# RWKV-7 low-rank products moved to two row halves of TensorE and two PSUM banks

## The chip, the cores and the metric

The kernel runs on one core of a Trainium2 chip. The metric is device microseconds of one execution. The engines are named as the profile names them: PE is TensorE, PEld its weight loads, ACT is ScalarE, DVE is VectorE, POOL is GpSimd and SP is SyncE, which issues most transfers. PSUM has eight banks of 512 fp32 columns; the code calls them bank 0 to bank 7.

## The reference, cut to what matters

The reference is one inference step of a two-layer decoder. Each layer projects its input once, runs three head groups on parts of the result (RG-LRU, RWKV-7 time mixing, latent attention), gates them, and projects back. The change touches only how RWKV-7 gets its decay and its gate `a`:

```python
w_log = -softplus(-(rk_w0 + tanh(xw @ rk_w1) @ rk_w2)) - 0.5
decay = exp(-exp(w_log))
a = sigmoid(rk_a0 + (xa @ rk_a1) @ rk_a2)
# per token t, with k, v, r, kk of the same token
s = s * decay + (s @ -kk) (kk * a)^T + v k^T
o = s @ r
```

Both are low-rank: 256 inputs go to 32 and from 32 to 256. There are 1104 tokens (1040 of one prompt with its meta tokens, 64 of eight samples), width 256, four heads of 64. All arithmetic is fp32.

## The kernel before, in words

Each layer is five blocks one after the other: `project_block`, `rwkv_block`, `prompt_block`, `sample_block`, `output_block`. Within a block each engine has its own instruction list, and the lists meet only in semaphores.

`project_block` computes the input projection (L406), tile of columns by tile of columns, in the order of the list `Z_JOBS`. ACT empties every tile from PSUM. Jobs named "front" are woven in, and they do the first steps of the first RWKV tile: "front" 0 has the first low-rank product (L468) and the key and receptance projections (L479), "front" 1 has the value projection (L479, into `aux[0]`, which is bank 6) and then the second low-rank products of decay and gate (L484, both into `aux[1]`, which is bank 7). ACT copies v out (L555) and takes one tanh over 512 columns (L557).

`rwkv_block` works on nine tiles of 128 tokens. A tile needs a chain of small products (the solve: `prod`, `n2`, `z1`, `z2`, `z3`, `mid`, `zf`, `wu`, `wt`), and a loop over four chunks of 32 tokens through the state: `read` k, an addition on DVE, `write` k, an update of the state on DVE (L1535), `read` k + 1. All engines walk through one order written by hand, `RWKV_ORDER`: behind each solve stage of tile t stand steps of neighbouring tiles, listed in `BESIDE`. Behind `prod` of tile t are the first low-rank product and the first projection of tile t + 1; behind `n2` are

```python
"n2": [("proj", 1, 1), ("lora", 1, 0), ("write", -1, 0)],
```

that is, the second projection of tile t + 1 (`proj`, L1020), the low-rank products of decay and gate of tile t + 1 (`lora`, L1026), and the first state write of tile t - 1 (`write`, L1207 and L1209, into columns 0 to 127 of bank 4). The tiles that `lora` handles here are 1 to 8; tile 0 comes from `project_block`.

`lora` takes from `low` two blocks of 32 rows, `tw[0:32, 0]` (tanh, for decay) and `tw[0:32, 1]` (a copy, for the gate), with a row of ones under each that adds the bias (`LORA + 1` = 33 rows). It multiplies them by `w2` and puts decay into columns 0 to 255 and gate into columns 256 to 511 of bank 7. ACT (L1269) turns the whole bank into `wa` with one tanh. DVE (`decay`, L1402 and L1403) makes `logd` and the gate of it, and `sums` multiplies `logd` by masks on PE.

The weights `w2` come in two loads of SyncE in `project_block` (L364, L365), counted by `m.s_ld` against `N_LD`.

Of the kernel before, what the change touches and what calls it, by code (L numbers as in the profile page):

```python
# [266 lines left out]
def project_block(nc, m):  # L267
# [39 lines left out]
    sq = {"ckv": mixed[:, 4:6, :], "cq": mixed[:, 2:4, :]}  # L307
    one = const[:, C_ONE * P:(C_ONE + 1) * P]
    N_PAR = 16 * 6
    N_LD = 16 * 6  # L310
    rw = rwkv_weights(m)

    def span(g):
# [6 lines left out]
    with nc.Block() as block:  # L320
        @block.sync
        def _(sp):
            def weights(i):
                if i >= 2:

                    sp.wait_ge(s_z, Z_LOADS[i - 1])
                w = z_weights(m, i)
                a = Z_AT[Z_LOADS[i]]
                sp.dma_start(w, m.w_z[layer, :, :, a:a + w.shape[2]]).then_inc(s_w[i], 16)

            if layer == 0:
                w0, n0 = z_weights(m, 0), Z_AT[2]
                for c in range(4):
                    k = slice(2 * c, 2 * c + 2)
                    sp.dma_start(xT[:, k, :], m.xT[:, k, :]).then_inc(m.s_x0[c], 16)
                    sp.dma_start(w0[:, k, 0:n0], m.w_z[0, :, k, 0:n0]).then_inc(m.s_x0[c], 16)
                sp.dma_start(w0[:, :, n0:], m.w_z[0, :, :, n0:Z_AT[Z_LOADS[1]]]).then_inc(m.s_const, 16)
            sp.dma_start(m.pfs[:, :], m.pf[layer]).then_inc(s_par, 16)
            sp.dma_start(lru_w, m.lru_w[layer]).then_inc(s_par, 16)
            sp.dma_start(slru, m.slru[layer]).then_inc(s_par, 16)  # L340
            sp.dma_start(shift, m.sshift[layer]).then_inc(s_par, 16)
            for b2 in range(2):
                sp.dma_start(ua_s[b2][:, :, 0:CX], m.sconv[layer, :, b2]).then_inc(s_par, 16)
            if layer == 0:
                sp.dma_start(const[:, :], m.consts[:, 0:C_N]).then_inc(m.s_const, 16)
                sp.dma_start(m.pages_in[:, :], m.pages_at).then_inc(m.s_const, 16)
            weights(1)
            weights(2)

            sp.wait_ge(s_ze, Z_TILES.index("ub1") + 1)  # L350
            n = 0
            for b2 in range(2):
                sp.dma_start(m.o_conv[layer, :, b2, 0:1, :], ua[:, b2, TP:TP + CX]
                             .rearrange("p (o t) -> p o t", o=1)).then_inc(s_out, 16)
                sp.dma_start(m.o_conv[layer, :, b2, 1:1 + NB, :], ua_s[b2][:, :, TS:TS + CX]).then_inc(s_out, 16)
                n += 2
            weights(3)
            sp.dma_start(rw.prow, m.prow[layer]).then_inc(m.s_ld, 16)
            sp.dma_start(rw.s_in, m.swkv[layer]).then_inc(m.s_ld, 16)
            sp.wait_ge(s_out, 16 * n)  # L360
            sp.wait_ge(s_xc, 2)
            sp.dma_start(rw.w1, m.rk_w1[layer]).then_inc(m.s_ld, 16)
            sp.dma_start(rw.rkw, m.rk_w[layer]).then_inc(m.s_ld, 16)
            sp.dma_start(rw.w2[0:LORA], m.rk_w2[layer]).then_inc(m.s_ld, 16)  # L364
            sp.dma_start(rw.w2[LORA:LORA + 1], m.prow[layer, LORA:LORA + 1, 0:2, :]).then_inc(m.s_ld, 16)  # L365
            sp.wait_ge(s_shift, 2)
            sp.dma_start(m.o_shift[layer], shend).then_inc(s_out, 16)
            sp.wait_ge(s_root, NG)
            sp.dma_start(m.o_ckv[layer], ckv[:, :, :]).then_inc(s_out, 16)
            sp.wait_ge(s_kr, 1)  # L370
            sp.dma_start(m.o_kr[layer], kr[64:64 + ROPE, :]).then_inc(s_out, 16)

            sp.wait_ge(s_h, 2)
            sp.dma_start(m.o_lru[layer], hend).then_inc(s_out, 16)

            sp.wait_ge(s_out, 16 * (n + 4))
# [25 lines left out]
        def _(pe):  # L402
# [19 lines left out]
            for job, i in Z_JOBS:  # L422
# [50 lines left out]
                if job == "front" and i < 2:  # L473
                    for n in ((0, 1), (2,))[i]:
# [5 lines left out]
                                                    rw.rkw[:, k, (1, 0, 2)[n], :], start=k == 0, stop=k == 1)  # L480
                        last.then_inc(s_rkv, 1)
                if job == "front" and i == 1:
                    for j in range(2):
                        last = nc.tensor.matmul(aux[1][:, j * WA:(j + 1) * WA], fw.tw[0:LORA + 1, j, :],  # L484
                                                rw.w2[0:LORA + 1, j, :], start=True, stop=True)
                    last.then_inc(s_lo2, 1)
                if job == "front" and i == 2:
                    pe.wait_ge(s_sg, 1)
# [11 lines left out]
        def _(act):  # L500
# [7 lines left out]
            for job, i in Z_JOBS:  # L508
# [35 lines left out]
                if job == "front" and i == 0:  # L544
                    act.wait_ge(s_lo1, 1)
                    nc.scalar.activation(fw.tw[0:LORA, 0, :], aux[1][0:LORA, 0:P], ACT.Tanh)
                    nc.scalar.copy(fw.tw[0:LORA, 1, :], aux[1][LORA:2 * LORA, 0:P]).then_inc(s_lo1e, 1)
                    act.wait_ge(s_rkv, 1)
                    nc.scalar.activation(fw.k_sb, aux[0][:, 0:WA], ACT.Copy,
                                         scale=const[:, C_ROW:C_ROW + 1]).then_inc(s_rkve, 1)  # L550
                    act.wait_ge(s_rkv, 2)
                    nc.scalar.copy(fw.r_sb, aux[1][:, 0:WA]).then_inc(s_rkve, 1)
                if job == "front" and i == 1:
                    act.wait_ge(s_rkv, 3)
                    nc.scalar.copy(fw.v_sb[:, 0], aux[0][:, 0:WA]).then_inc(s_rkve, 1)  # L555
                    act.wait_ge(s_lo2, 1)
                    nc.scalar.activation(fw.wa, aux[1], ACT.Tanh, scale=0.5).then_inc(s_lo2e, 1)  # L557
                if job == "front" and i == 2:
                    act.wait_ge(s_kk, 1)
                    for h in range(H_B):  # L560
# [34 lines left out]
        def _(dve):  # L595
# [110 lines left out]
            def both(x):  # L706
                return x.rearrange("p (o n) -> p o n", o=1).to_broadcast([P, 2, WA])

            nc.vector.memset(fw.tw[LORA:LORA + 1, :, :], 1.0)
            a = PF["mix"][0]  # L710
            link(nc.vector.tensor_scalar(fw.rest, m.pfs[:, a:a + 10], -1.0, 1.0, ALU.mult, ALU.add))
            dve.wait_ge(m.s_ld, N_LD)
# [36 lines left out]
SOLVE = ["prod", "n2", "z1", "z2", "z3", "mid", "zf", "wu", "wt"]  # L749
BESIDE = {  # L750
    "prod": [("low", 1, 0), ("read", -1, 0), ("proj", 1, 0), ("norm", -2, 0)],
    "n2": [("proj", 1, 1), ("lora", 1, 0), ("write", -1, 0)],
    "z1": [("read", -1, 1), ("proj", 1, 2), ("decay", 1, 0), ("centre", -2, 0)],
    "z2": [("write", -1, 1), ("sums", 1, 0), ("finish", -2, 0)],
    "z3": [("read", -1, 2), ("keys_norm", 1, 0)],
# [37 lines left out]
def rwkv_block(nc, m):  # L793
# [156 lines left out]
            if stage in stages:  # L950
                stages[stage](t, k)

    N_LD = 16 * 6
    with nc.Block() as block:
        @block.sync
        def _(sp):
# [40 lines left out]
        def _(pe):  # L997
# [25 lines left out]
            def lora(t, _):  # L1023
                pe.wait_ge(s_lo1e, t + 1)
                for i in range(2):
                    last = nc.tensor.matmul(bank[7][:, i * WA:(i + 1) * WA], tw[0:LORA + 1, i, :], w2[0:LORA + 1, i, :],  # L1026
                                            start=True, stop=True)
                last.then_inc(s_lo2, 1)

# [151 lines left out]
            def write(t, k):  # L1181
                if k >= len(steps(t)):
                    return
                n = steps_to(t) + k
                pe.wait_ge(s_u, n + 1)
                pe.wait_ge(s_hat, t + 1)
                if n >= 1:
                    pe.wait_ge(s_state, n + 1)
                if of_samples(t, k):
                    pe.wait_ge(s_pl, 2)  # L1190
                    pe.wait_ge(s_um, 1)
                    pe.wait_ge(s_wu, RT)
                    for hf in range(2):
                        for i, x in enumerate((um, vm)):
                            for c in range(2):
                                for p in range(2):
                                    last = nc.tensor.matmul(
                                        bank[4 + c][64 * p:64 * p + 64, hf * 2 * P:(hf + 1) * 2 * P],
                                        bk[rows(2 + c), t % 3, i, head(hf, p)], x[rows(2 + c), :, head(hf, p)],
                                        start=i == 0, stop=i == 1)  # L1200
                    last.then_inc(s_wr, 1)
                    return
                for i, c in enumerate(steps(t)[k]):
                    for hf in range(2):
                        for p in range(2):
                            out = bank[4][64 * p:64 * p + 64, i * P + hf * HD:i * P + (hf + 1) * HD]
                            nc.tensor.matmul(out, bk[rows(c), t % 3, 0, head(hf, p)],  # L1207
                                             u[rows(c), hf, p * HD:(p + 1) * HD], start=True, stop=False)
                            last = nc.tensor.matmul(out, bk[rows(c), t % 3, 1, head(hf, p)],  # L1209
                                                    v_sb[rows(c), t % 3, head(hf, p)], start=False, stop=True)  # L1210
                    last.then_inc(s_wr, 1)
# [31 lines left out]
        def _(act):  # L1243
            bank = m.bank

            def low(t, _):
                act.wait_ge(s_lo1, t + 1)
                nc.scalar.activation(tw[0:LORA, 0, :], bank[7][0:LORA, 0:P], ACT.Tanh)
                nc.scalar.copy(tw[0:LORA, 1, :], bank[7][LORA:2 * LORA, 0:P]).then_inc(s_lo1e, 1)

            def proj(t, n):
                act.wait_ge(s_rkv, 3 * t + n + 1)
# [12 lines left out]
            def lora(t, _):  # L1265
                act.wait_ge(s_lo2, t + 1)
                if t >= 1:
                    act.wait_ge(s_sg, t)
                nc.scalar.activation(wa, bank[7], ACT.Tanh, scale=0.5).then_inc(s_lo2e, 1)  # L1269

            def sums(t, _):
                act.wait_ge(s_kk, t + 1)
# [1359 lines left out]
```

## Time and profile before

| | |
|---|---|
| median of three runs | 2076.92 us (2073.3 to 2080.65) |
| the profiled execution | 2072.72 us, span 2070.9 us |
| PE / PEld busy over the span | 93% / 60% |
| DVE / ACT / POOL busy | 50% / 31% / 11% |
| projection block, layers 0 and 1 | about 0 to 282 and 1040 to 1320 us |
| RWKV block, layers 0 and 1 | about 282 to 470 and 1320 to 1510 us |
| mean granted PE clock | 0.975 of full speed |

The span runs from the first to the last instruction. A fp32 matmul of the program shows as two MATMUL rows (and two LDWEIGHTS rows) in the trace, so a count of 4 at L1026 is one pair of products. The duration of a MATMUL row includes the time for which it flows through the array and overlaps with the next row, so the time that a group takes from PE is read from its start to the start of the next group. Tiles of the program that live in the one large buffer all appear as `work`, and so groups are told apart by their lines.

### The profile page before, as it was taken

The numbers are of one execution on the slowest core, as the hardware profiler recorded it, in microseconds if no ns is written. First come the engines' busy times: TensorE is split into PE (matmuls) and PEld (weight loads), VectorE is DVE, ScalarE is ACT, GpSimd is POOL, SyncE is SP. The second block draws the span as 40 slices with busy tenths as digits, with TensorE's granted clock in tenths as the row PEclk, the third lists the DMA queues.
The fourth block names the chain that finished last, engine by engine and source line by source line (L and its number), as shares of the span: only waits on it lengthen the run. The fifth ranks groups of instructions, "written<-read, shape, count | busy, mean of one in ns | idle before, by whom it ended". The sixth has DMA issues, their size and how long they took to land. (4 is left out here: it accounts for less than half of the span.)

```text
span 2070.9 us, 50992 instructions
## 1 busy us (share of the span) xinstructions
PE 1934.8 (93%) x22434; PEld 1248.1 (60%) x22434; DVE 1031.0 (50%) x2399; ACT 643.5 (31%) x1711; POOL 223.2 (11%) x223
## 2 busy tenths in 40 slices
PE   8999989988999999999989999899889999999997
PEld 5665667775566567754446656677755665677443
DVE  2017127775566468833330071277755664688333
ACT  1222234442455432310012222344424554322000
POOL 0000001010000034202100000001100000442022
PEclk9999999997999989999999999999979999999999
DMA  6102010000000367731121020100000002677121
GB/s 213 51 1 91 1 48 4 4 4 23 1 1 10 83 232 270 260 129 61 67 64 51 1 92 0 48 4 4 4 23 1 1 14 79 244 272 266 62 81 53
DMA packets 50112, 151.13 MB, mean 73 GB/s; under 512 B 15138, under 2 KB 19490, under 8 KB 40420
## 3 DMA queue, kind: packets, MB, share of 16 engines
q1 hardware_dynamic: 37604, 72.36, 10.5%
q0 software_dynamic: 12288, 75.51, 9.8%
q8 instruction: 178, 2.92, 0.6%
q14 instruction: 42, 0.34, 0.1%
HBM read 130.27 MB, written 12.86 MB: 69 GB/s over the span
## 5 line engine op out<-in xcount | busy, mean ns | idle before, releaser
L406 PE MATMUL psum<-work 128*128 128x368 f32 x1536 | 484.6, 476 | 8.9 <-DMA work<-w_z 6.6
L406 PEld LDWEIGHTS psum<-work 128*128 128x128 f32 x1536 | 293.6, 192 | 193.7 <-issue 8.2
L2465 PE MATMUL psum<-work,mixed 128*128 128x512 f32 (+1 forms) x576 | 248.8, 592 | 1.6 <-PEq L2137 1.6
L2465 PEld LDWEIGHTS psum<-work,mixed 128*128 128x128 f32 (+1 forms) x576 | 106.2, 186 | 137.7 <-issue 137.7
L2333 DVE STREAM_TRANSPOSE work<-work 128x1024 f32<-128x1024 f32 x128 | 150.5, 1214 | 0.3 <-issue 0.2
L1906 ACT ACTIVATE work<-psum,work 128x128 f32<-128x128 f32 (+8 forms) x130 | 98.0, 754 | 160.6 <-DVE work L2015 160.4
L1786 PE MATMUL psum<-work 96*128 96x512 f32 (+3 forms) x384 | 139.1, 495 | 2.3 <-ACT work L1906 2.1
L2077 POOL DMA_INDIRECT work<-cache_ckv,pages x64 | 60.7, 948 | 606.9 <-PE psum L1740 377.7
L2237 PE MATMUL psum<-work,ckv 128*64 128x256 f32 x1024 | 117.6, 382 | 0.7 <-ACT ckv L2292 0.7
L2513 DVE SCALAR_TENSOR_TENSOR work<-work,psum 128x512 f32<-128x512 f32 (+1 forms) x36 | 23.1, 683 | 162.1 <-PE psum L2465 162.1
L1786 PEld LDWEIGHTS psum<-work 96*128 96x128 f32 x384 | 67.4, 189 | 60.0 <-issue 43.5
L2014 DVE TENSOR_REDUCE work<-psum 128x1 f32<-128x128 f32 (+8 forms) x130 | 99.5, 765 | 4.5
L651 DVE TENSOR_TENSOR mixed<-work 128x1104 f32<-128x1104 f32 x4 | 5.2, 1307 | 193.6 <-ACT work L579 193.5
L1797 PE MATMUL psum<-const_sb,work 128*128 128x128 f32 x594 | 84.9, 276 | 13.7 <-ACT work L1915 13.1
L2237 PEld LDWEIGHTS psum<-work,ckv 128*64 128x64 f32 x1024 | 71.6, 137 | 42.8 <-issue 11.3
L1915 ACT COPY work<-psum 128x512 f32<-128x512 f32 (+1 forms) x166 | 84.2, 546 | 23.3 <-PE psum L1797 22.5
L1797 PEld LDWEIGHTS psum<-const_sb,work 128*128 128x128 f32 x594 | 67.0, 141 | 38.9 <-issue 18.2
L1733 PE MATMUL psum<-cq,work 128*128 128x368 f32 x192 | 72.6, 510 | 11.1 <-DVE work L1965 7.6
L1815 PE MATMUL psum<-work 128*64 128x128 f32 x1152 | 81.9, 280 | 0.0
L2013 DVE TENSOR_TENSOR psum<-psum,const_sb 128x128 f32<-128x128 f32 (+1 forms) x130 | 38.2, 294 | 87.3 <-PE psum L1786 72.7
L523 ACT ACTIVATE mixed<-psum 128x368 f32<-128x368 f32 x48 | 19.4, 477 | 183.3 <-PE psum L406 183.3
L2282 ACT ACTIVATE work<-psum,work 128x1024 f32<-128x1024 f32 x32 | 35.7, 1115 | 130.5 <-DVE work L2344 130.5
(311 smaller groups left out, 2953.0 us busy)
## 6 DMA issues: line engine op xcount, KB each, us to landing
work<-w_z SPq DMA_DIRECT2D x4, 2560.0 KB, 11.0
work<-w_out SPq DMA_DIRECT2D x4, 2048.0 KB, 8.8
xres<-work SPq DMA_DIRECT2D x16, 512.0 KB, 2.9
work<-xT SPq DMA_DIRECT2D x4, 1104.0 KB, 8.8
work<-x_tok SPq DMA_DIRECT2D x8, 512.0 KB, 4.0
work<-xres SPq DMA_DIRECT2D x8, 512.0 KB, 4.3
work<-w_z SPq DMA_DIRECT2D x1, 2304.0 KB, 13.9
o_ckv<-ckv SPq DMA_DIRECT2D x2, 1104.0 KB, 4.3
```

The source lines that it names most:

```text
L406: return nc.tensor.matmul(zb[i % 2][n][:, 0:G], z_weights(m, g)[:, k, lo:lo + Z_W[i]], xT[:, k, span(n)], start=k == 0, stop=k == DK - 1)
L1733: last = nc.tensor.matmul(bank_of(j)[:, 0:G], wuq[:, k, h, :], cq[:, k, span(g)], start=k == 0, stop=k == 1)
L1786: last = nc.tensor.matmul(m.bank[2 * u + b][:, 0:w], qt[0:96, p % 2, u, t * P:(t + 1) * P], kt[0:96, p % 2, u, a:a + w], start=True, stop= ...
L1797: last = nc.tensor.transpose(m.bank[4 + at % 2][0:w, n * P:(n + 1) * P], pr[:, i % 2, u * N_FULL * P + c * P:u * N_FULL * P + c * P + w], ...
L1815: last = nc.tensor.matmul(m.bank[6][u * VD:(u + 1) * VD, 0:P], val[:, c, (2 * p + u) * VD:(2 * p + u + 1) * VD], pT[:, i % 2, n * P:(n + 1 ...
L1906: nc.scalar.activation(pr[:, i % 2, u * N_FULL * P:u * N_FULL * P + keys(i)], scores_of(i, u), ACT.Exp, bias=mx[:, 2 * (i % 2) + u:2 * (i ...
L1915: nc.scalar.copy(pT[0:w, i % 2, 4 * g * P:(4 * g + len(c)) * P], m.bank[4 + at % 2][0:w, 0:len(c) * P]).then_inc(s_pte, 1)
L2014: link(nc.vector.tensor_reduce(sm, scores_of(i, u), AX, ALU.max))
L2077: pool.indirect_dma_start(rows[n % RING][:, s, :], None, m.cache_ckv, row).then_inc(m.s_pg[n % RING], 16)
L2237: last = nc.tensor.matmul(m.bank[6 + n % 2][64 * s:64 * s + 64, 0:R], pT[:, n % 2, j, 64 * s:64 * s + 64], pgc[n % RING][:, s, j * R:(j + ...
L2333: last = nc.vector.transpose(kt[:, half, s], pgc[n % RING][:, s, :].rearrange("p (j k n) -> p j k n", j=KEYS, k=2) [:, :, half, :])
L2465: last = nc.tensor.matmul(yb[t % 2][half][0:n, :], m.mixed[:, k, lo:lo + n], wo[half][:, k, :], start=k == 0, stop=k == DK - 1)
```

## The change

The two low-rank products get different rows of the array and different banks. The gate's operands (`tw[..., 1, :]` and `w2[..., 1, :]`, with the row of ones and the bias row) move from partitions 0 to 32 to partitions 64 to 96. Decay's product stays in bank 7, columns 0 to 255; the gate's goes to columns 256 to 511 of another bank: bank 4 in `rwkv_block`, `aux[0]` (bank 6) in `project_block`. From this follow:

- Tanh is taken in two passes of 256 columns instead of one of 512.
- `w2` and its bias row arrive in four loads instead of two, and the memset of ones is two.
- In `project_block`, PE waits before the pair until ACT has copied k, r and v out (`s_rkve` 3), since v is read from the bank that the gate's product writes.
- In `rwkv_block`, the first state write of a tile (k = 0, bank 4) waits until the tanh of the low-rank products issued before it is done (`s_lo2e`), and `lora` now stands before the second projection in the order.

```diff
-    N_LD = 16 * 6
+    N_LD = 16 * 8
...
-            sp.dma_start(rw.w2[0:LORA], m.rk_w2[layer]).then_inc(m.s_ld, 16)
-            sp.dma_start(rw.w2[LORA:LORA + 1], m.prow[layer, LORA:LORA + 1, 0:2, :]).then_inc(m.s_ld, 16)
+            for j in range(2):
+                r = 2 * LORA * j
+                sp.dma_start(rw.w2[r:r + LORA, j], m.rk_w2[layer, :, j]).then_inc(m.s_ld, 16)
+                sp.dma_start(rw.w2[r + LORA:r + LORA + 1, j], m.prow[layer, LORA:LORA + 1, j, :]).then_inc(m.s_ld, 16)
...
                 if job == "front" and i == 1:
+                    pe.wait_ge(s_rkve, 3)
                     for j in range(2):
-                        last = nc.tensor.matmul(aux[1][:, j * WA:(j + 1) * WA], fw.tw[0:LORA + 1, j, :],
-                                                rw.w2[0:LORA + 1, j, :], start=True, stop=True)
+                        r = slice(2 * LORA * j, 2 * LORA * j + LORA + 1)
+                        last = nc.tensor.matmul(aux[1 - j][:, j * WA:(j + 1) * WA], fw.tw[r, j, :],
+                                                rw.w2[r, j, :], start=True, stop=True)
...
-                    nc.scalar.activation(fw.wa, aux[1], ACT.Tanh, scale=0.5).then_inc(s_lo2e, 1)
+                    for j in range(2):
+                        w = slice(j * WA, (j + 1) * WA)
+                        last = nc.scalar.activation(fw.wa[:, w], aux[1 - j][:, w], ACT.Tanh, scale=0.5)
+                    last.then_inc(s_lo2e, 1)
...
-            nc.vector.memset(fw.tw[LORA:LORA + 1, :, :], 1.0)
+            for j in range(2):
+                nc.vector.memset(fw.tw[2 * LORA * j + LORA:2 * LORA * j + LORA + 1, j, :], 1.0)
...
-    "n2": [("proj", 1, 1), ("lora", 1, 0), ("write", -1, 0)],
+    "n2": [("lora", 1, 0), ("proj", 1, 1), ("write", -1, 0)],
...
             def lora(t, _):
                 pe.wait_ge(s_lo1e, t + 1)
                 for i in range(2):
-                    last = nc.tensor.matmul(bank[7][:, i * WA:(i + 1) * WA], tw[0:LORA + 1, i, :], w2[0:LORA + 1, i, :],
+                    r = slice(2 * LORA * i, 2 * LORA * i + LORA + 1)
+                    last = nc.tensor.matmul(bank[(7, 4)[i]][:, i * WA:(i + 1) * WA], tw[r, i, :], w2[r, i, :],
                                             start=True, stop=True)
...
+                if k == 0:
+                    pe.wait_ge(s_lo2e, min(t + 3, RT))
...
-                nc.scalar.copy(tw[0:LORA, 1, :], bank[7][LORA:2 * LORA, 0:P]).then_inc(s_lo1e, 1)
+                nc.scalar.copy(tw[2 * LORA:3 * LORA, 1, :], bank[7][LORA:2 * LORA, 0:P]).then_inc(s_lo1e, 1)
...
-                nc.scalar.activation(wa, bank[7], ACT.Tanh, scale=0.5).then_inc(s_lo2e, 1)
+                for i in range(2):
+                    w = slice(i * WA, (i + 1) * WA)
+                    last = nc.scalar.activation(wa[:, w], bank[(7, 4)[i]][:, w], ACT.Tanh, scale=0.5)
+                last.then_inc(s_lo2e, 1)
```

## Rows read from the trace of the kernel before

**Rows 1.** Busy time of each engine in the RWKV block, layer 0; granted clock

```profile
core 0: us, PE busy (x) PEld busy (x) DVE busy (x) ACT busy (x) POOL busy (x), PEclk, DMA share, GB/s
...
282.00:470.00 188.00, 169.54 (x5250) 136.78 (x5240) 131.56 (x460) 86.97 (x301) 17.42 (x16) 0.97 0.04 14
```

**Rows 2.** Timeline of one RWKV tile, layer 0: start, us, engine, line

```profile
306.07 1.13 PE L1020 MATMUL psum<-work 128*128 128x256 f32 x4
306.18 0.37 ACT L1315 COPY work<-psum 128x256 f32<-128x256 f32 x1 [0.18 <-PE psum L1089]
...
307.13 1.13 PE L1026 MATMUL psum<-work 33*128 33x256 f32 x4
...
308.19 0.34 PE L1207 MATMUL psum<-work 32*64 32x64 f32 x4
308.29 0.60 ACT L1269 ACTIVATE work<-psum 128x512 f32<-128x512 f32 x1 [0.68 <-PE psum L1026]
```

**Rows 3.** PE by line and shape: count, busy us, mean ns

```profile
L2465 PE MATMUL psum<-work,mixed 128*128 128x512 f32 x512 | 221.2, 592 | 1.6 <-PEq L2137 1.6
L2237 PE MATMUL psum<-work,ckv 128*64 128x256 f32 x1024 | 117.6, 382 | 0.7 <-ACT ckv L2292 0.7
...
L2206 PE MATMUL psum<-work,ub 32*64 32x256 f32 x2048 | 66.6, 396 | 0.0
...
L1026 PE MATMUL psum<-work 33*128 33x256 f32 x64 | 18.0, 402 | 0.0
```

**Rows 4.** Timeline of the same tile: state reads whose halves differ in rows

```profile
303.54 0.31 PE L1171 MATMUL psum<-work 64*32 64x64 f32 x4
...
303.68 0.28 PE L1174 MATMUL psum<-work 64*32 64x64 f32 x4
...
303.79 0.30 PE L1171 MATMUL psum<-work 64*32 64x64 f32 x4
```

**Rows 5.** Timeline: narrow products in two row halves; ScalarE copies before them

```profile
321.62 1.07 ACT L1292 COPY work<-psum 128x512 f32<-128x512 f32 x2 [0.30 <-PE psum L1053]
...
322.75 0.86 PE L1065 MATMUL psum<-work 64*32 64x64 f32 x64 [0.51 <-ACT work L1292]
...
323.54 1.09 PE L1006 MATMUL psum<-ub,work 128*64 128x128 f32 x8
```

**Rows 6.** Timeline: four ScalarE passes over 256 columns of PSUM

```profile
314.46 1.21 ACT L1282 ACTIVATE work<-psum 128x256 f32<-128x256 f32 x4 [1.52 <-PE psum L1043]
```

**Rows 7.** What PE waits for, layer 0 from 288 to 456 us

```profile
PE psum L1020 <- DVE work L1460: 5.9, 6, 1.0
```

**Rows 8.** Projection block, layer 0, around its low-rank products: timeline

```profile
202.86 0.27 DVE L709 MEMSET work<- 1x256 f32 x1
...
204.98 1.67 DVE L702 SCALAR_TENSOR_TENSOR work<-work,pfs,ub 128x128 f32<-128x128 f32 x6
...
211.07 1.09 PE L468 MATMUL psum<-ub,work 128*64 128x128 f32 x8
...
229.66 1.03 PE L479 MATMUL psum<-work 128*128 128x256 f32 x4
229.86 1.22 ACT L523 ACTIVATE mixed<-psum 128x368 f32<-128x368 f32 x3 [14.47 <-PE psum L406]
...
230.61 1.13 PE L484 MATMUL psum<-work 33*128 33x256 f32 x4
230.95 0.39 ACT L555 COPY work<-psum 128x256 f32<-128x256 f32 x1
...
231.67 4.60 PE L406 MATMUL psum<-work 128*128 128x368 f32 x14
```

**Rows 9.** SyncE: issue of a small load; a wait behind it

```profile
L364 SPq DMA_DIRECT2D work<-rk_w x2: 429/444/460, 161.5 to 1200.0; - x2
...
SPq L369 <- DVE ckv L663: 9.6, 1, 9.6
```

**Rows 10.** Projection block, ScalarE loading a function table

```profile
248.99 1.28 ACT L567 ACT_TABLE_LOAD   x1
```

More of the change, by code:

```diff
@@ L546, in _ @@
                     nc.scalar.activation(fw.tw[0:LORA, 0, :], aux[1][0:LORA, 0:P], ACT.Tanh)
-                    nc.scalar.copy(fw.tw[0:LORA, 1, :], aux[1][LORA:2 * LORA, 0:P]).then_inc(s_lo1e, 1)
+                    nc.scalar.copy(fw.tw[2 * LORA:3 * LORA, 1, :], aux[1][LORA:2 * LORA, 0:P]).then_inc(s_lo1e, 1)
                     act.wait_ge(s_rkv, 1)
@@ L951, in run @@
                 stages[stage](t, k)
-    N_LD = 16 * 6
+    N_LD = 16 * 8
     with nc.Block() as block:
```

## Prediction

> **What bounds the kernel now.** I read the page first, then the busy time by stretch, then the waits of the stretch that the change touches, then the timeline of one tile in it, and last the timeline of the projection block, where the same pair of products stands once per layer. The reader is to see four things.
>
> In the RWKV block TensorE (PE) is busy for 169.5 of 188 us, and no other engine for more than 131.6 [rows 1]. PE runs one hand-written order, so whatever shortens that order shortens the block, unless a wait further on belongs to another engine's own chain. The decay's and gate's products (L1026) take a PE slot of 308.19 - 307.13 = 1.06 us and nothing else runs in it [rows 2]. A trace row is half of an fp32 product: four rows for two products. Per row, 512 columns take 221.2 / 512 = 0.432 us, so 256 columns take 0.216 [rows 3]. Four of these are 0.864; the other 0.19 us of the slot is the first weight load and the array running empty at its end, and the projection slot beside it (306.07 to 307.13) has the same 1.06 [rows 2]. There are 64 rows of L1026, so 16 pairs in the kernel, eight per layer [rows 3].
>
> **Saved: do the two products overlap?** Before, both use array rows 0 to 32 and write bank 7. Afterwards they stand in rows 0 to 32 and 64 to 96 and write banks 7 and 4. No row of this trace shows two row halves with 128 output columns each, so the gain is bounded from nearby rows. For it: L2206 (32 rows, 64 columns out, 256 in; 2048 rows of that form) takes 66.6 / 2048 = 0.033 us per row against 0.216 alone, 6.6 times less. Column halves alone, as in L2237, give 117.6 / 1024 = 0.115, under 2 times less. So the four row quarters of L2206 do overlap, writing four banks [rows 3]. Row halves in particular: the state reads L1171 and L1174 alternate in the code between the halves and write two banks; the 8 rows from 303.54 to 303.79 take 0.25 us, 0.031 each, where 64 columns alone cost 0.432 / 8 = 0.054 [rows 4]. That is four steps of 0.0625 instead of 0.054, 0.009 lost per step. I take full overlap with that loss: two steps of 0.216 in place of four, 0.432 - 0.02 = **0.41 us saved per pair**, a slot of 0.65. Upper end: no loss, 0.43. Lower end: L1065 is also in row halves, and its 64 rows start over 323.54 - 322.75 = 0.79 us, 0.0123 each, far above 0.054 / 8. Something per row, taken here as the weight load of 64 x 32, is paid one after another there [rows 5]. Four times the columns is 0.05; two of those before the second product starts are 0.10, which leaves 0.33 saved.
>
> A rule is to be weighed here. The rows above show four rows of L1171 (both halves) ahead of four rows of L1174, though the code issues L1171 and L1174 of one half before those of the other; the two halves are interleaved [rows 4]. The Trainium skill ("TensorE: Matmul & The Clock Gate", Part 3, what overlaps and what doesn't) says that matmuls are a strict queue in start and end, without reordering. Read for an fp32 product of two passes, it would let only the first product's second pass run beside the second's first. By the row, two steps are saved; by the rule, one, which is the second rival below.
>
> **Does the saving reach the end?** After the pair come the projection (now behind it), the first state write, z1, the state read and so on. From 306.07 on, PE has no gap until after L1207 [rows 2]. The PE waits further on are short and come from DVE or ACT work which itself follows PE work behind this slot: the largest, L1020 on DVE L1460, is 5.9 us in 6 tiles [rows 7]. DVE's queue up to L1460 goes back through the state updates and reads to the first state write, so the chain and the wait move earlier together. I take all of it: 16 x 0.41 = 6.6 us.
>
> **The new wait of the first state write.** It must wait until both tanh passes are done, because the second product now lies in bank 4 beside the write. Swapping the order puts the projection's 1.06 us between. In tile time: the pair starts at 306.07 and the projection at 306.07 + 0.65 = 306.72. ACT took up the old tanh at 308.29, 0.10 after PE's next slot began, so the new one at 306.82; ACT is free from 306.18 + 0.37 = 306.55 [rows 2]. Two passes over 256 columns: four take 1.21 us [rows 6] and one about 0.37 (the copy of rows 2), so each further one 0.28; two take 0.65, against 0.60 for the one of 512 columns. They end at 307.47, and PE learns it 0.06 later: L1292 ends at 321.62 + 1.07 = 322.69 and L1065 starts at 322.75 [rows 5]. That is 307.53. PE reaches the write at 306.72 + 1.06 = 307.78. Cost 0 with 0.25 us of cover. Were the cover gone, each us of lateness would cost one per tile, since the write, z1 and every read behind it stand in PE's queue, and DVE's state update waits for the write. The projection's copy on ACT follows tanh and its product ends later anyway: 0. Before and after, the stretch has three changes of product shape, and the 0.19 us around a slot was the same for the projection and the pair: 0.
>
> **The projection block.** There the new wait is not covered. PE finishes the value projection (L479) and went on to the pair at 230.61. Now it waits for ACT's copy of v (L555), since the second product goes to the bank which that copy reads. The copy stands behind three gate passes (229.86 + 1.22) and ends at 230.95 + 0.39 = 231.34, plus 0.06 = 231.40: **0.79 us of wait** [rows 8]. The pair then saves 0.41. PE is dense on both sides (L406 follows at 231.67), so net +0.38 per layer, **+0.76** in all. If the pair saves 0.33 to 0.43 it is +0.92 to +0.72.
>
> **Loads and small edits, at nothing.** The low-rank weights arrive in four loads instead of two, so two more issues of 0.43 us on SyncE, and the wait behind them there (output of ckv) lasts 9.6 us anyway [rows 9]. They are issued near 162 us and DVE first uses the weights after 202.86. One memset of 0.27 us becomes two, 0.27 more at most; DVE's preparation ends at 204.98 + 1.67 = 206.65 and PE's first product of it starts at 211.07 [rows 8]. The gate's copy to other partitions keeps its shape.
>
> **Sum.** -6.6 + 0.76 = -5.8 us. With the bounds of the pair: -16 x 0.33 + 0.92 = -4.4 to -16 x 0.43 + 0.72 = -6.2. The profiled execution took 2072.72 us (span 2070.9), so it would take 2066.9. The median of the runs shown, 2076.92, is 4.2 above it, and the same step gives **2071.1** (-0.28%), own range 2070.7 to 2072.5 before scatter; the three runs of before lie up to 3.7 us from their median.
>
> **Rivals.**
> A, the forecast: both steps overlap and all reaches the end. 0.72.
> B, one step only, by program order: 0.22 saved per pair, 16 x 0.22 = 3.5, less 2 x (0.79 - 0.22) = 1.1: -2.4, 2074.5. For it, that no row has 128 columns out in halves; against it, the interleaving [rows 4]. 0.10. (It is also what the page's rule above would give.)
> C, overlap, but the gain is taken back by a wait on DVE: L1020's wait of 1.0 us per tile [rows 7] would grow by 0.41. It would if DVE's chain crossed this slot without touching PE; DVE waits for the first state write, so I see no such chain. 16 x 0.41 gone, +0.76 stays: 2077.7. 0.08.
> D, no overlap at all, as if 128-column products took the whole array: nothing saved, 2 x 0.79 = +1.6: 2078.5. The L2206 row speaks against it [rows 3]. 0.04.
> E, the other side: the state write waits because tanh comes late. It needs ACT to be over 0.25 us later than worked out; the gain is gone at 0.25 + 5.8 / 16 = 0.61 late. Price by a row: a function table load of 1.28 us before tanh [rows 10], 1.03 of stall per tile, 16 x 1.03 - 5.8 = +10.7: 2087.6. Against it: ACT does tanh and copies back to back in this block without such a load [rows 2]. 0.06, half of it for a smaller lateness which only eats the gain.
>
> **How the numbers follow.** About 0.3% (6.2 us) is what a measurement of this kernel can tell from no change. A lies just inside it, so with a scatter of one or two us it falls outside some 45 times in 100: 0.72 x 0.45 = 0.32, and 0.01 from B. Slower by over 0.3%: half of E, 0.03, and 0.02 for scatter on C and D. The rest, 0.62, is within. The range takes A with the runs' scatter below, 2066.5, and reaches over B, C and D above, 2078.5.
>
> **What would show it.** In the profile after: rows of L1026's successor in pairs that start together, its slot at about 0.65 and the tile period shorter by 0.41; the first state write with no idle time ahead of it that ACT releases; in the projection block PE idle about 0.8 us ahead of the pair, released by ACT's copy of v. Wrong would be: a slot of 0.84 (B) or 1.06 (D); PE idle ahead of the write (E); a larger wait on DVE L1460's counterpart with the same period (C).

## The result, and the profile after

| | before | after |
|---|---|---|
| median, first 20 runs each | 2078.82 us | 2072.01 us (2064.13 to 2081.76) |
| ratio after / before, with 95% interval | | 0.9963 (0.9952 to 0.9975) |
| the same kernel again, 12 runs beside 20 of before | 2078.18 us | 2076.18 us, ratio 0.9986 (0.9972 to 1.0000) |
| the profiled execution | 2072.72 us | 2076.18 us, span 2074.4 us |

The change makes the kernel slightly faster. The forecast was -5.8 us, 0.9972. The first comparison says 0.37% less and the second 0.14%; the forecast lies between them, inside the first interval and at the edge of the second. A step of a quarter of a per cent is about as large as the difference between two such series, so its size is read from the traces, piece by piece.

The profiled execution itself is of no use as a total: it is 3.5 us longer than the one of before, the third slowest of its kernel's twenty. Up to the last pair of low-rank products it is ahead (1470.2 against 1476.6 us). Its excess lies in the last 600 us, where almost nothing was changed: from that pair to the end it takes 2074.4 - 1470.2 = 604.2 us, and before it was 594.3. The mean granted clock of this stretch is 0.95 of full speed against 0.97, and 0.02 of 600 us is 12 us (an estimate from two rounded clocks), which is as much as the excess. One such place is near 1932 us, where PE ran at the lower of its two clocks (0.51, against 1.00 at the same place before). Busy time by stretch, after (the number before the last two is the granted clock):

```profile
1470.20:2074.40 604.20, 559.27 (x5961) 345.61 (x5955) 334.10 (x696) 181.42 (x462) 94.60 (x89) 0.95 0.27 94
...
1932.00:1942.00 10.00, 9.13 (x32) 4.89 (x33) 1.56 (x8) 0.00 (x0) 0.00 (x0) 0.51 0.51 197
```

and before:

```profile
1476.64:2070.90 594.26, 550.69 (x5952) 339.52 (x5951) 333.83 (x695) 181.17 (x460) 93.80 (x88) 0.97 0.27 96
...
1938.00:1948.00 10.00, 10.00 (x24) 4.40 (x24) 0.00 (x0) 0.00 (x0) 0.00 (x0) 1.00 0.37 151
```

**One tile of the RWKV block**, timeline of PE after (L1028 is the projection that was L1020, L1035 the pair that was L1026, L1218 the first state write that was L1207):

```profile
306.09 0.67 PE L1098 MATMUL psum<-work 32*32 32x64 f32 x32
306.69 0.70 PE L1035 MATMUL psum<-work 33*128 33x256 f32 x4
307.32 1.13 PE L1028 MATMUL psum<-work 128*128 128x256 f32 x4
308.38 0.34 PE L1218 MATMUL psum<-work 32*64 32x64 f32 x4
...
328.31 0.49 PE L1035 MATMUL psum<-work 33*128 33x256 f32 x2
```

The reader is to see the pair's slot, 307.32 - 306.69 = 0.63 us where it was 1.06 [rows 2], and no idle time in front of the write at 308.38. The tile takes 328.31 - 306.69 = 21.62 us. Before, from 307.13 [rows 2] to the same place of the next tile (timeline of PE before):

```profile
329.17 1.13 PE L1026 MATMUL psum<-work 33*128 33x256 f32 x4
```

22.04 us. So 0.42 us per tile arrives whole at the next tile. Both are the shortest steps of their traces, and several tiles are up to 0.7 us longer in either kernel. Over the six steps of each layer from the second pair to the eighth, the mean falls from 22.16 to 21.76 us, by 0.40. ACT in the same tile, after: copy of the solve's second product, the two tanh passes, copy of the projection.

```profile
306.80 0.37 ACT L1329 COPY work<-psum 128x256 f32<-128x256 f32 x1 [0.19 <-PE psum L1098]
307.44 0.66 ACT L1282 ACTIVATE work<-psum 128x256 f32<-128x256 f32 x2 [0.27 <-PE psum L1035]
308.49 0.37 ACT L1270 COPY work<-psum 128x256 f32<-128x256 f32 x1 [0.39 <-PE psum L1028]
```

Tanh ends at 308.10 and the write may start 0.06 later; PE gets there at 308.38, with 0.22 to spare. What PE waits for, after, layer 0 from 288 to 456 us:

```profile
PE psum L1028 <- DVE work L1474: 5.9, 6, 1.0
PE psum L1074 <- ACT work L1306: 3.8, 8, 0.5
```

The wait for DVE is as long as in [rows 7]: it has moved with the tile and has not grown.

**The projection block**, timeline of PE and of ACT's copy of v after:

```profile
214.30 1.10 PE L481 MATMUL psum<-work 128*128 128x256 f32 x4 [0.66 <-ACT work L553]
...
230.08 1.03 PE L481 MATMUL psum<-work 128*128 128x256 f32 x4
231.81 0.70 PE L488 MATMUL psum<-work 33*128 33x256 f32 x4 [0.71 <-ACT work L559]
232.45 5.83 PE L408 MATMUL psum<-work 128*128 128x368 f32 x18
```

```profile
231.37 0.39 ACT L559 COPY work<-psum 128x256 f32<-128x256 f32 x1
```

From the value projection to the next column tile it is 232.45 - 230.08 = 2.37 us, where it was 231.67 - 229.66 = 2.01 [rows 8]: +0.36 per layer, of which the wait is 0.78 (the pair starts 1.73 after the projection instead of 0.95) and the shorter pair -0.42.

### The profile page after: what moved, and what is told of

It is laid out like the page before. It is cut to its first block and busy times, and to the rows that moved or that the text cites. A ratio compares the mean times of both kernels' runs of the same rounds, so it can differ in the third digit from the quotient of the medians.

```text
span 2074.4 us, 51032 instructions
## 1 busy us (share of the span) xinstructions
PE 1938.1 (93%) x22434; PEld 1249.6 (60%) x22434; DVE 1030.8 (50%) x2401; ACT 644.3 (31%) x1729; POOL 223.0 (11%) x223
```

## The experiments

Eight experiments. The ratios are to the kernel before on the same chip, with 95% intervals; the first four share one chip, and the last four another.

### Banks, order and waits without the row halves

```diff
-                        r = slice(2 * LORA * j, 2 * LORA * j + LORA + 1)
+                        r = slice(0, LORA + 1)
...
-                    r = slice(2 * LORA * i, 2 * LORA * i + LORA + 1)
+                    r = slice(0, LORA + 1)
```

(loads, memset and the gate's copy follow)

> Everything of the change but the row halves: both products stay in rows 0 to 32, with two banks, two tanh passes, the swapped order and both waits. My theory (the gain is the overlap of row halves): PE slot of a pair 1.06 us again, tile period 22.04, no idle time of PE ahead of the first state write, about 0.8 us of it ahead of the pair in the projection block; in all 2 x 0.78 = +1.6 us, ratio to before 1.0008. Rival (two banks alone, or the order with the projection behind the pair, shorten the tile): period below 22.04 and a ratio near 0.9965, as the full change.

Measured: 2080.02 us, ratio 1.0006 (0.9994 to 1.0019). Two tiles of its RWKV block, PE:

```profile
1434.86 1.13 PE L1035 MATMUL psum<-work 33*128 33x256 f32 x4
1435.91 1.13 PE L1028 MATMUL psum<-work 128*128 128x256 f32 x4
1436.97 0.34 PE L1218 MATMUL psum<-work 32*64 32x64 f32 x4
...
1456.90 1.13 PE L1035 MATMUL psum<-work 33*128 33x256 f32 x4
```

Slot 1.05, period 22.04, no idle time ahead of the write. In the projection block PE idles ahead of the pair for ACT, as in the full change. Banks, order and two tanh passes bring nothing without the row halves; the gain needs them. No run has the row halves with a single bank, so whether the second bank is needed is not shown.

### The pair behind the second projection again

```diff
-    "n2": [("lora", 1, 0), ("proj", 1, 1), ("write", -1, 0)],
+    "n2": [("proj", 1, 1), ("lora", 1, 0), ("write", -1, 0)],
```

> The full change, but the pair stands behind the second projection again, right ahead of the first state write that waits for its tanh. Theory: the swap is what hides the wait. Tanh starts 0.75 us after the pair does, lasts 0.66, and 0.06 later PE may write: 1.47 us after the pair's start, where PE is free at 0.63, so 0.83 us idle in each of 7 tiles a layer; against before +0.41 in 14 tiles, -0.42 in the two tiles without such a write, +0.72 in the projection blocks: +5.6 us, ratio 1.0027, period 22.45. Rival (the wait costs nothing wherever the pair stands, since the state chain on DVE is later anyway): period 21.62 and a ratio near 0.9965.

Measured: 2098.21 us, ratio 1.0106 (1.0088 to 1.0124), about +22 us (20.3 between the medians): the direction that was expected, and about four times the size. The idle time is right. PE in one tile, and the wait over layer 0:

```profile
306.92 0.70 PE L1035 MATMUL psum<-work 33*128 33x256 f32 x4
...
329.44 0.70 PE L1035 MATMUL psum<-work 33*128 33x256 f32 x4
330.99 0.34 PE L1218 MATMUL psum<-work 32*64 32x64 f32 x4 [0.85 <-ACT work L1282]
...
333.10 2.07 PE L1028 MATMUL psum<-work 128*128 128x256 f32 x4
...
353.41 0.70 PE L1035 MATMUL psum<-work 33*128 33x256 f32 x4
```

```profile
PE psum L1218 <- ACT work L1282: 6.0, 7, 0.9
```

But the next projection takes 2.07 us instead of 1.13. The stretches show why (busy time by stretch, one tile):

```profile
326.00:332.60 6.60, 5.28 (x166) 3.97 (x168) 2.96 (x18) 2.36 (x7) 1.01 (x1) 1.00 0.01 2
332.60:336.00 3.40, 3.40 (x81) 2.40 (x75) 1.78 (x7) 0.79 (x3) 0.00 (x0) 0.50 0.02 5
336.00:350.00 14.00, 12.65 (x398) 10.57 (x386) 11.93 (x36) 7.48 (x29) 1.17 (x1) 1.00 0.01 4
```

After the wait of 0.99 us for DVE and, some 4 us later, the new one of 0.85, the granted clock fell from 2.4 to 1.2 GHz for 3.4 us. Of the 14 tiles with the new wait, 12 have the wait of 0.99 some 4 us ahead of it, and 9 of these 12 were followed by such a stretch (the pairs at 329, 353, 377, 401, 1377, 1401, 1425, 1449 and 1473 us; not those at 425, 448 and 1497). The two tiles with the 0.85 alone (307 and 1354 us) were not. After the full change, with the wait of 0.99 but without the other, the clock stayed at 1.00 over twelve tiles:

```profile
306.70:437.20 130.50, 119.05 (x3737) 96.12 (x3732) 98.83 (x350) 63.01 (x224) 12.20 (x12) 1.00 0.02 4
1339.60:1470.20 130.60, 119.31 (x3731) 96.39 (x3730) 98.79 (x350) 62.99 (x224) 12.18 (x12) 1.00 0.02 4
```

So the two waits together go with the lower clock, though not every time; why three tiles were spared is open. A 3.4 us stretch of busy PE at half clock holds 1.7 us of work, so it costs about 1.7. The period is 353.41 - 329.44 = 23.97 us; 22.45 was expected without this, and the difference of 1.5 is that stretch: the one before it (306.92 to 329.44), without such a stretch after its waits, took 22.52. With it, 5.6 + 9 x 1.5 = 19.1 us are accounted for of the 20 to 22.

### The value projection earlier

```diff
-                    for n in ((0, 1), (2,))[i]:
+                    for n in ((0, 1, 2), ())[i]:
                         if n >= 1:
                             pe.wait_ge(s_lo1e, 1)
-                            pe.wait_ge(s_rkve, n)
+                            pe.wait_ge(s_rkve, 1)
```

(ACT's copy of v moves to front 0 with it)

> The full change, and the value projection of the first tile moves from front 1 to the end of front 0, so that its copy is long done when the pair asks for the bank. Theory (PE's wait of 0.78 us per layer ahead of the pair is all lost time, since PE is dense on both sides): no idle time of PE there, -1.6 us against the full change, and against before -16 x 0.42 - 2 x 0.42 = -7.6 us, ratio 0.9963 if the full change were -6.0. Rival (the time comes back elsewhere, as the wait for ACT at the end of front 0 grows): idle time ahead of the next column tile of 0.5 us or more per layer, and no gain against the full change.

Measured: 2071.61 us, ratio 0.9973 (0.9961 to 0.9984), against 0.9963 and 0.9986 for the full change: a difference of 1.6 us can't be told from these. The trace can. PE:

```profile
211.75 1.13 PE L481 MATMUL psum<-work 128*128 128x256 f32 x4
213.54 1.97 PE L481 MATMUL psum<-work 128*128 128x256 f32 x8 [0.66 <-ACT work L553]
215.34 15.00 PE L408 MATMUL psum<-work 128*128 128x368 f32 x48
230.27 0.70 PE L488 MATMUL psum<-work 33*128 33x256 f32 x4
230.91 5.52 PE L408 MATMUL psum<-work 128*128 128x368 f32 x17
```

The pair follows the column tile without idle time. From the receptance projection to the end of the pair's slot it is 230.91 - 213.54 = 17.37 us; with the full change it was 232.45 - 214.30 = 18.15. So 0.78 is back per layer and the wait at the end of front 0 stays 0.66: that rival falls.

### Each product in two pieces

```diff
+                    for q in range(2):
+                        last = nc.tensor.matmul(bank[(7, 4)[i]][:, i * WA + q * P:i * WA + (q + 1) * P], tw[r, i, :],
+                                                w2[r, i, q * P:(q + 1) * P], start=True, stop=True)
```

> The full change, but each product of the RWKV block is issued as two of 128 columns, in the order decay, decay, gate, gate. Theory 1 (the array takes work for the two row halves from separate queues, as the state reads suggest): rows of decay and gate still start in pairs, slot of the pair about 0.65 us or 0.02 more, time as the full change. Theory 2 (matmuls start strictly in issue order, two passes of one product one after the other, and only neighbours overlap): decay's four rows of 0.108 us first and only the last beside the gate's first, 7 steps: slot 0.95, +0.32 us per tile, +5.1 us against the full change, ratio to before about 0.999.

PE:

```profile
306.66 0.72 PE L1036 MATMUL psum<-work 33*128 33x128 f32 x8
307.31 1.13 PE L1028 MATMUL psum<-work 128*128 128x256 f32 x4
```

The slot is 0.65 us for eight rows. In issue order it would have been 0.95 by the estimate above. The rows also start in pairs, 13 ns apart; in the first 0.04 us two have started (timeline cut at 306.70 us):

```profile
306.66 0.39 PE L1036 MATMUL psum<-work 33*128 33x128 f32 x2
```

A row does not name its row half, but in the kernel before, with both products in one half, the four rows of a pair start 0.22 us or more apart. So the second piece of decay did not hold back the first of the gate: work for the two row halves ran side by side, across whole instructions. Whether the array or the instruction stream put the rows in that order is not shown. The Trainium skill ("TensorE: Matmul & The Clock Gate", Part 3, what overlaps and what doesn't) has matmuls in strict order in start and end. This slot does not fit that, if the rows are issued in the order of the kernel's calls.

The time does not follow, however: 2079.60 us, ratio 1.0018 (1.0005 to 1.0031), 7 to 11 us above the full change's two series, where the slot explains 16 x 0.02. The mean granted clock of its runs, 0.972, lies between those of the two series (0.973 and 0.971), so the clock does not explain it. Its tiles are 21.64 us at best in layer 0, but 21.82 to 22.64 in layer 1. One place seen there: the z2 products (64 rows) take longer than in the full change, 0.92 us from start to start instead of 0.68, with no semaphore behind it. This kernel, then the full change:

```profile
1417.36 0.99 PE L1086 MATMUL psum<-work 32*32 32x32 f32 x64
1418.28 0.34 PE L1219 MATMUL psum<-work 32*64 32x64 f32 x4
```

```profile
1431.65 0.75 PE L1085 MATMUL psum<-work 32*32 32x32 f32 x64
1432.33 0.34 PE L1218 MATMUL psum<-work 32*64 32x64 f32 x4
```

In layer 1 these products take 0.86 to 1.26 us in every tile of this kernel, and 0.68 in six of seven after the full change: 2.0 us in all. Why they take longer, and the rest of the difference, is not settled.

### The pair in PE's longest wait

```diff
-    "prod": [("low", 1, 0), ("read", -1, 0), ("proj", 1, 0), ("norm", -2, 0)],
-    "n2": [("lora", 1, 0), ("proj", 1, 1), ("write", -1, 0)],
+    "prod": [("low", 1, 0), ("read", -1, 0), ("lora", 1, 0), ("proj", 1, 0), ("norm", -2, 0)],
+    "n2": [("proj", 1, 1), ("write", -1, 0)],
```

> The full change, but the pair moves from the n2 stage into the prod stage, between the state read and the first projection, where PE waits 0.99 us for DVE in 12 tiles. Its operands are ready when the read ends, so it takes its 0.63 us out of that wait, and its tanh is done long before the first state write. Theory (PE's order bounds the block, and that wait is DVE's own chain, which doesn't move): the wait falls to about 0.36 us, tile period 21.62 - 0.63 = 20.99, -7.6 us against the full change; against before -6.0 - 7.6 = -13.6 us, ratio 0.9935. Rival (DVE's chain up to that wait follows PE's place in the tile, so the wait stays 0.99 and only moves): period 21.62 and a ratio near 0.997, or the waits of the solve grow by what is saved.

Measured: 2066.28 us, ratio 0.9948 (0.9929 to 0.9967). PE at two tiles, and its wait over layer 0 (280 to 460 us):

```profile
325.97 0.70 PE L1035 MATMUL psum<-work 33*128 33x256 f32 x4
```

```profile
346.96 0.70 PE L1035 MATMUL psum<-work 33*128 33x256 f32 x4
347.91 1.10 PE L1028 MATMUL psum<-work 128*128 128x256 f32 x4 [0.25 <-DVE work L1474]
```

```profile
PE psum L1028 <- DVE work L1474: 1.0, 4, 0.3
```

Period 346.96 - 325.97 = 20.99 us, as worked out, and the wait of 0.99 is 0.25 (0.36 expected). From the state read to the projection it is 347.91 - 346.26 = 1.65 us, and after the full change it was 348.02 - 346.37 = 1.65. So the wait belonged to DVE's chain, which did not move.

### Both

The last diff and the early value projection together.

> The kernel with the pair in the wait, and the value projection of the first tile in front 0 as well. Theory: both are PE time on the path and add up, -1.6 us more, -15.2 us against before, ratio 0.9927. Rival: the second brings nothing that reaches the end, ratio as with the pair in the wait alone.

Measured: 2062.98 us, ratio 0.9932 (0.9911 to 0.9953), the fastest here by its median. The step from the run before, 0.0016, is less than the intervals; again the pair follows the column tile without idle time in the projection block.

### The kernel before with the pair in that wait

```diff
-    "prod": [("low", 1, 0), ("read", -1, 0), ("proj", 1, 0), ("norm", -2, 0)],
-    "n2": [("proj", 1, 1), ("lora", 1, 0), ("write", -1, 0)],
+    "prod": [("low", 1, 0), ("read", -1, 0), ("lora", 1, 0), ("proj", 1, 0), ("norm", -2, 0)],
+    "n2": [("proj", 1, 1), ("write", -1, 0)],
```

> The kernel before (rows 0 to 32 for both, one bank, one tanh, no new waits), with its pair moved to the same place in the prod stage. Theory: the slot of 1.06 us fills the wait of 0.99 and shows 0.05 to 0.1 beyond it, so about 0.94 us in 13 tiles: -12.2 us against before, ratio 0.9941: most of what the row halves and the place give together, without row halves. Rival (the wait is not DVE's alone, and a pair of 1.06 there delays squares and solve): ratio near 1.

Measured: 2067.11 us, ratio 0.9948 (0.9930 to 0.9966). PE at two tiles:

```profile
323.60 1.13 PE L1026 MATMUL psum<-work 33*128 33x256 f32 x4
324.66 1.13 PE L1020 MATMUL psum<-work 128*128 128x256 f32 x4
...
344.73 1.13 PE L1026 MATMUL psum<-work 33*128 33x256 f32 x4
```

Period 344.73 - 323.60 = 21.13 us, 0.91 less than before (0.94 expected). The old pair with its full slot of 1.06, merely put where PE was idle, gives more than twice what the row halves give in the old place (0.42). These are again the shortest steps; by the mean of the same twelve steps it is 0.78 against 0.40. With the pair in the wait, the row halves add only 21.13 - 20.99 = 0.14 us per tile, and the times of the two kernels, 2066.28 and 2067.11 us, can't be told apart.

### The change again

> The changed kernel itself, to lay beside the others on one chip. Theory: -16 x 0.42 + 2 x 0.36 = -6.0 us against before, ratio 0.9971. Rival (something beyond the slots helps, such as fewer stretches at the lower clock): ratio 0.9963 or less again, with tiles and projection no shorter than in the trace at hand.

Measured: 2076.18 us, ratio 0.9986 (0.9972 to 1.0000). Against the first series (0.9963) this shows how far two series of one kernel lie apart. -6.0 us (0.9971) is inside the first interval and just outside the second (0.9972 to 1.0000); nothing calls for a further gain. The two series differ in their clock: their means are 2071.99 us at a granted clock of 0.9730 and 2074.57 at 0.9712, and within the series of this document a run is about 1.3 us longer per 0.001 of clock less. That is 2.3 of the 2.6 us. Brought to one clock in the same way, the change is some 4.5 us faster than the 20 runs of before beside it (2077.42 us at 0.9726), an estimate.

## Why the prediction was right

- **The overlap (rival A against B and D).** 0.41 us per pair forecast, 0.42 to 0.43 measured; the slot is 0.63, not 0.84 or 1.06. With the row halves taken out, the gain is gone. The choice near the upper bound was right: 128 output columns in each half overlap as well as the narrow ones did, and the weight loads that gave the lower bound of 0.33 don't show.
- **The saving reaches the end of the tile (against C).** Period 22.04 to 21.62, the wait on DVE unchanged at 0.99.
- **The new wait of the state write (against E).** Forecast 0 with 0.25 us of cover; measured 0 with 0.22. The experiment without the swap shows the price if the cover is gone, and here the reasoning was short: "each us of lateness would cost one per tile" left out the clock. With 0.85 us of idle time a tile lost 2.35 us against the full change, 1.5 of them to the lower clock. Rival E's price, 1.03 us of stall per tile and no more, was too low for the same reason.
- **The projection block.** 0.79 of wait and +0.38 net forecast, 0.78 and +0.36 measured, and taking the wait away gave 0.78 back.
- **Loads, memset, the second tanh pass.** Forecast nothing; two tanh passes take 0.66 us against the 0.65 worked out, and no wait on the loads appears.

The terms as measured, -16 x 0.42 + 2 x 0.36 = -6.0 us, stand beside the forecast of -5.8. The first series' 0.9963 would be -7.7; the 1.7 us between show in no piece of the trace, and the second series, 0.9986 or -2.9, errs to the other side. The whole time alone would not have decided: -2.9 is nearer to rival B's -2.4 than to the forecast. The slot and the tile step decide for A. That the first median came within 1 us of the forecast 2071.1 is partly luck, since that series lies 6.8 us under its own before and the second 2.0. The prediction also gave a change under 0.3% about twice the chance of a gain over it; the first series (0.37%) is over that line and the second (0.14%) under.

## What to carry to other kernels

Two products of 33 rows each that stand in different halves of the array and write different banks cost PE little more than one, and the saving reaches the end if PE's order is what bounds the stage; but price the waits that the second bank brings, since one here (0.78 us, twice) took back a fifth of the gross gain. Look at PE's idle time before making a product cheaper: the same pair moved as it was into a wait of 0.99 us saved 0.91 per tile, overlapping it in a full stretch saved 0.42, and both together 1.05, so the one leaves little for the other. And a wait's price is not its length alone when other short waits are near.

## What the runs showed of the hardware

- Two short idle times of PE in one tile (0.99 and 0.85 us, some 4 us apart) were followed by 3.4 us at a granted clock of 0.50 in 9 of 12 tiles; with the 0.99 alone the clock stayed at 1.00 over twelve tiles.
- Products of two row halves ran side by side across whole instructions: decay, decay, gate, gate of 128 columns took 0.65 us, where issue order would give 0.95 (an estimate from the rows).
- Two fp32 products of 33 rows and 256 columns took 0.63 us together in two row halves, and 1.05 to 1.06 in one, whether they wrote one bank or two.
- One kernel's runs differ by up to 0.85% (2064.13 to 2081.76 us), and the granted clock goes with them: the fastest of the 20 runs after had 0.978, the slowest 0.967, about 1.3 us per 0.001 over all series.
